# Hybrid pooling and attention block: shift eighths at steps 11 to 26, V's bias by one-column products, w_out's quarters in another order

## What is computed

```python
mod = silu_c @ w_ada[l] + b_ada[l]                      # (B, 6D)
sh_m, sc_m, gt_m, sh_f, sc_f, gt_f = jnp.split(mod[:, None, :], N_MOD, axis=-1)
h = rmsnorm(x, g_pre_mix[l]) * (1 + sc_m) + sh_m
hc = rmsnorm(ctx, g_pre_mix[l]) * (1 + scc_m) + shc_m
p, q1, q2, k1, k2, v = project(h, w_in[l])
...
attn = diff_attend_blocked(q1, q2, k1_all, k2_all, v_all, lam)
attn = rmsnorm(attn, g_subln[l]) * (1 - lambda_init)
pool = pool_mixer(p, w_pool[l], pool_scale[l])
mix = jnp.concatenate([pool, attn.reshape(b, n, ATTN_WIDTH)], axis=-1) @ w_out[l]
x_new = x + gt_m * rmsnorm(mix, g_post_mix[l])
h2 = rmsnorm(x_new, g_pre_ffn[l]) * (1 + sc_f) + sh_f
x_new = x_new + gt_f * rmsnorm(swiglu(h2, w_gate_up[l], w_down[l]), g_post_ffn[l])
```

## Time and profile before

| | us |
|---|---|
| median of 3 runs | 1827.84 (1826.86 to 1827.89) |
| profiled execution, its own time | 1834.15 |
| its span, slowest core (2) | 1832.6 |
| spans of the 8 cores | 1820.8 to 1832.6 |
| TensorE busy | 1731.5 |
| VectorE, ScalarE, GpSimd busy | 624.0, 511.2, 133.0 |

### The profile page before, as it was taken

How to read it: one execution, slowest core, us unless ns; L and a number is a source line. 1 busy time by engine, 2 the same in 40 slices (tenths; PEclk the granted TensorE clock), 3 DMA queues, 4 the chain that set the end, 5 groups by cost and what they waited for, 6 DMA issues and landing times.

```text
span 1832.6 us, 28161 instructions; the slowest of 8 cores (1820.8 to 1832.6 us)
## 1 busy us (share of the span) xinstructions
PE 1731.5 (94%) x11377; PEld 889.6 (49%) x11377; DVE 624.0 (34%) x1360; ACT 511.2 (28%) x794; POOL 133.0 (7%) x147
## 2 busy tenths in 40 slices
PE   1389999999999999989999999999999999999998
PEld 1245545545567676644444444444444444444443
DVE  2124576677545454545521232231110110101023
ACT  2044210000499999925520000000000000101011
POOL 1000000000010111100001111100000000000000
PEclk9599999999999999999999999999999999999999
DMA  9988961045436758674599789757467643544556
GB/s 190 164 205 210 182 116 23 1 63 88 84 60 113 137 96 140 107 147 151 144 163 114 96 114 126 99 75 112 60 81 92 79 86 64 88 70 74 85 146 230
DMA packets 153615, 205.10 MB, mean 112 GB/s; under 512 B 3312, under 2 KB 129680, under 8 KB 146576
## 3 DMA queue, kind: packets, MB, share of 16 engines
q0 software_dynamic: 144368, 145.24, 54.4%
q1 hardware_dynamic: 9120, 58.06, 9.7%
HBM read 331.72 MB, written 16.79 MB: 190 GB/s over the span
## 4 chain that ended last, share of the span: by engine, by line
PE 88%; DMA 6%; another core or an unknown queue 3%; DVE 1%; ACT 1%; issue 1%; SPq 0%; DVEq 0%; POOL 0%; ACTq 0%; POOLq 0%
PE ps L315 87%; DMA arena<-xa 2%; DMA arena<-w_out 2%; PE ps L319 1%; DMA arena<-w_ada 1%; DMA arena<-w_dn 1%; ACT arena L288 1%; DVE arena L298 0%; DVE arena L303 0%; ACT sml L288 0%; DVE arena L306 0%; DVE arena L294 0%; SPq L322 0%; DVE sml L309 0%
## 5 line engine op out<-in xcount | busy, mean ns | idle before, releaser
L315 PE MATMUL ps<-arena 128*128 128x512 bf16 (+2 forms) x9547 | 1683.0, 338 | 20.5 <-DMA arena<-w_out 6.2
L315 PEld LDWEIGHTS ps<-arena 128*128 128x128 bf16 x9547 | 811.7, 98 | 845.8 <-issue 100.7
L288 ACT ACTIVATE arena<-ps 128x1024 bf16<-128x1024 f32 (+5 forms) x500 | 395.3, 838 | 1125.0 <-PE ps L315 1122.4
L294 DVE TENSOR_TENSOR arena<-arena,ps 128x512 bf16<-128x512 f32 (+1 forms) x90 | 61.1, 679 | 491.2 <-PE ps L315 489.9
L303 DVE SCALAR_TENSOR_TENSOR arena<-arena,sml 128x128 f32<-128x128 f32 (+3 forms) x239 | 120.0, 527 | 47.4 <-POOL sml L789 20.8
L294 DVE TENSOR_TENSOR arena<-ps,arena 128x512 f32<-128x512 f32 (+1 forms) x81 | 54.6, 674 | 230.5 <-ACT arena L288 212.0
L294 DVE TENSOR_TENSOR arena<-arena 128x512 f32<-128x512 f32 (+7 forms) x128 | 113.9, 890 | 9.2 <-DVE arena L303 1.4
L319 PE MATMUL ps<-identsb,arena 128*128 128x128 bf16 x499 | 42.2, 232 | 45.4 <-DVE arena L298 28.4
L315 PE MATMUL ps<-cpair,arena 128*128 128x1 bf16 (+1 forms) x1280 | 57.5, 164 | 27.4 <-DMA arena<-w_ada 27.4
L322 POOL DMA_DIRECT2D arena<-w_gu x44 | 50.5, 1150 | 423.5 <-PE ps L315 423.5
L288 ACT ACTIVATE arena<-arena 128x2048 bf16<-128x2048 f32 x27 | 51.5, 1908 | 81.7 <-DVE arena L294 43.2
(11 more groups left out here) (53 smaller groups left out, 225.9 us busy)
## 6 DMA issues: line engine op xcount, KB each, us to landing
arena<-w_gu POOLq DMA_DIRECT2D x44, 1024.0 KB, 14.1
arena<-w_ada POOLq DMA_DIRECT2D x32, 1024.0 KB, 13.2
arena<-xa SPq DMA_DIRECT2D x27, 1024.0 KB, 10.9
arena<-w_dn POOLq DMA_DIRECT2D x16, 1408.0 KB, 11.1
arena<-w_in POOLq DMA_DIRECT2D x6, 2048.0 KB, 19.6
arena<-w_ada POOLq DMA_DIRECT2D x4, 2048.0 KB, 51.3
arena<-w_out POOLq DMA_DIRECT2D x4, 2048.0 KB, 18.0
xscr<-arena SPq DMA_DIRECT2D x8, 1024.0 KB, 4.8
```

The lines of the kernel that those rows point to most:

```text
L288: P.op("act", lambda e: e.activation(out, in_, func, **kw), rd, wr)
L294: P.op("dve", lambda e: e.tensor_tensor(out, a, b, op), [a, b], [out])
L315: P.op("pe", lambda e: e.matmul(out, lhsT, rhs, start=start, stop=stop, skip_group_check=skip), [lhsT, rhs], [out], signal=signal)
```

## The change

1. The eighths of the shift stand behind steps 11, 12, 15, 17, 19, 21, 23 and 26. The x load of tile 6 waits for the third quarter of V's weights only.
2. V's bias: 128 products of one column (the shift as one bf16 column per kc, V's weights stationary) write 8 columns of bank 6. These are scaled, split into three bf16 parts, transposed behind head 0 of K, summed on 8 partitions, stored to DRAM and loaded as a row on all partitions into `bvrow`.
3. The late pool products move from steps 0, 3, 5, 7, 9 of the attention to steps 4, 6, 8, 10, 12, 14; no units of `fill` stand in the first round. So the last unit stands in round 14 behind its step 9, not its step 3. The fifth exponential buffer and the mixer gate's row `GT_m` move to free places.
4. For tile 0 the output projection takes quarters 2, 1, 3 for all four column blocks and then quarter 0; the other tiles take 2, 1, 3, 0 within each block.

```diff
-            dma("sp", xs, xa[i * 128:(i + 1) * 128, :], after=[V_AB[:, 12:16, :]] if late else ())
+            dma("sp", xs, xa[i * 128:(i + 1) * 128, :], after=[V_AB[:, 8 if i == 6 else 12:12 if i == 6 else 16, :]] if late else ())
...
-        shq = {13 + 2 * e: e for e in range(8)}
+        shq = {s_: e for e, s_ in enumerate((11, 12, 15, 17, 19, 21, 23, 26))}
...
-        def bias_v(c2, wslot, b):
-            for kc in range(16):
-                mm(bank(b), shrep[:, kc, :], wslot[:, kc, :], kc == 0, kc == 15, signal=(kc == 15))
-            cp(bvt[:, c2 * 512:(c2 + 1) * 512], bank(b))
+        def bias_v(c2, wslot):
+            for h in range(4):
+                for kc in range(16):
+                    mm(bank(6)[:, 4 * c2 + h:4 * c2 + h + 1], wslot[:, kc, h * 128:(h + 1) * 128], shc[:, kc:kc + 1],
+                       kc == 0, kc == 15, signal=(h == 3 and kc == 15), skip=True)
+
+        def bias_row():
+
+            ts(bcol, bank(6)[:, 0:8], sc1(S_LAM + 6), None, ALU.mult)
+            for k in range(3):
+                cp(bpart[:, k, :], bcol)
+                if k < 2:
+                    tt(bcol, bcol, bpart[:, k, :], ALU.subtract)
+
+        def bias_store():
+            v = bankbf(4)
+            for k in range(3):
+                tp(v[0:8, k * 128:(k + 1) * 128], bpart[:, k, :], signal=(k == 2))
+            cp(brow[0:8, :], v[0:8, 256:384])
+            tt(brow[0:8, :], brow[0:8, :], v[0:8, 128:256], ALU.add)
+            tt(brow[0:8, :], brow[0:8, :], v[0:8, 0:128], ALU.add)
+            P.dma("sp", lambda e: e.dma_start(out=bvs[0].rearrange("(c p) -> c p", p=128), in_=brow[0:8, :]),
+                  [brow[0:8, :]], [("bv", 0)])
...
-        ts(bvrow, bvt, sc1(S_LAM + 6), None, ALU.mult)
+        dma("sp", bvrow, bvs[0].partition_broadcast(128), rd=[("bv", 0)])
...
-            if g == 0:
-                pool_mm(1, (2,), late=True)
             PV(g)
-            if g == 0:
-                pool_mm(1, (3,), late=True)
-            if g in (3, 5, 7, 9):
-                pool_mm(0, [(g - 3) // 2], late=True)
+            if g in (4, 6):
+                pool_mm(1, [g // 2], late=True)
+            if g in (8, 10, 12, 14):
+                pool_mm(0, [g // 2 - 4], late=True)
...
-            if (it > 0 and 3 <= kc <= 13) or (it == 0 and kc > 11):
+            if it > 0 and 3 <= kc <= 13:
                 fill(1)
...
-        def o_mm(t, n):
-            for kc in range(16):
-                mm(bank(ob(t, n)), mixT(kc)[:, t * 128:(t + 1) * 128], w_o[kc // 4][:, kc % 4, n * 512:(n + 1) * 512],
-                   kc == 0, kc == 15, signal=(kc == 15))
+        WQ = (2, 1, 3, 0)
+
+        def o_mm(t, n, qs=WQ):
+            for q in qs:
+                for k in range(4):
+                    mm(bank(ob(t, n)), mixT(4 * q + k)[:, t * 128:(t + 1) * 128], w_o[q][:, k, n * 512:(n + 1) * 512],
+                       q == WQ[0] and k == 0, q == WQ[3] and k == 3, signal=(k == 3))
...
+        for q in WQ[:3]:
+            for n in range(4):
+                o_mm(0, n, (q,))
         for t in range(8):
             for n in range(4):
-                o_mm(t, n)
+                o_mm(t, n, WQ if t else WQ[3:])
```

More of the change, by code:

```diff
@@ L212, in build_nc @@
     xscr = nc.dram_tensor("xscr", [NOWN, D], F32, kind="Internal").ap()
+    bvs = nc.dram_tensor("bvs", [1, 1024], F32, kind="Internal").ap()
     gts = nc.dram_tensor("gts", [2, D], F32, kind="Internal").ap()
@@ L238, in build_nc @@
         P.space("gt", 2, 1)
+        P.space("bv", 1, 1)
         def region(off, nelem, dt):
@@ L484, in add_shift @@
                 ts(o, o, modc[:, 16 + kc:17 + kc], None, ALU.add)
-        shrep = region(KT0, 16 * 128, BF16).rearrange("p (c m) -> p c m", c=16)
-        bvt = region(X0 + 16384, 1024, F32)
-        def bias_v(c2, wslot, b):
-            for kc in range(16):
-                mm(bank(b), shrep[:, kc, :], wslot[:, kc, :], kc == 0, kc == 15, signal=(kc == 15))
-            cp(bvt[:, c2 * 512:(c2 + 1) * 512], bank(b))
+        shc = sc1(244, 8).bitcast(BF16)
+        bcol = sml2[:, 128:136]
+        bpart = sml2[:, 136:148].bitcast(BF16).rearrange("p (k c) -> p k c", k=3)
+        brow = sml2[:, 160:288]
+        def bias_v(c2, wslot):
[18 more added lines that the diff above has]
+                  [brow[0:8, :]], [("bv", 0)])
         gsub = sml2[:, 0:128]
@@ L536, in build_nc @@
             if s == 31:
-                cp(shrep, modc[:, 16:32].unsqueeze(2).to_broadcast([128, 16, 128]))
+                cp(shc, modc[:, 16:32])
             if 28 <= s < 32:
@@ L545, in build_nc @@
             if s == 33:
-                bias_v(0, V_A, 6)
+                bias_v(0, V_A)
                 dma("sp", ropt, rope_d.rearrange("j p t -> p j t"))
             if s == 34:
-                bias_v(1, V_B, 3)
+                bias_v(1, V_B)
+        bias_row()
         add_shift(hT_oth, 0, 256)
@@ L597, in build_nc @@
                 turned(KT[:, h, k0:k0 + n], w, h % 4, src, lo, n, tok)
+            if h == 0:
+                bias_store()
         dma("pool", Q_1, w_in_v[:, :, 1536:2048])
@@ L683, in build_nc @@
         load_ada(3)
-        pbuf = [region(o, 1024, BF16) for o in (HW + 16384, HW + 18432, HW + 20480, HW + 22528, X0 + 23040)]
-        GT_m = region(HW + 24576, 2048, F32)
+        pbuf = [region(o, 1024, BF16) for o in (HW + 16384, HW + 18432, HW + 20480, HW + 22528, HW + 24576)]
+        GT_m = region(X0, 2048, F32)
         GT_f = region(X0, 2048, F32)
```

## The result

The changed kernel takes 1823.84 us (median of 10 runs, 1822.02 to 1825.63), the kernel before 1827.87 in the same runs: ratio 0.9977 (95% interval 0.9968 to 0.9986), 4.0 us less. Forecast were 15.7 less, in a range of 8 to 23 less.

A forecast was written before the change was run, and what follows sets the result against it. TensorE was taken as the bound, working nearly all the time, so only its work or few idle gaps pay. Terms -8.1 - 3.1 - 2.0 - 2.5 = -15.7 us took the median 1827.84 to 1812; range 1805 to 1820.

The forecast's parts named there:

- Part 1: Output projection's head: new order of w_out's quarters removes the 6.17 us wait and low clock; -8.1 us.
- Part 2: V's bias: 128 one-column products at 27 ns replace 32 products of 512 columns; net -3.1 us.
- Rival (c): V's bias: one-column products cost 98 ns each, +9.0 us on the forecast, 1821 us; chance 0.05.
- Part 3: Attention's head: later pool products and moved fills remove ScalarE's 2.51 us pause at exponential 4; -2.0 us.
- Part 4: V's projection: earlier eighths of the shift and earlier x tile of chain 6; -2.5 us, from -9 to +6.
- I take -0.5: V's projection: x tile fetched after the third weight quarter delays the fourth but brings the transposes forward; -0.5 us.
- I take -2.0: V's projection: eighths issued earlier use half-idle DMA engines and shorten TensorE's waits and low clock; -2.0 us.
- rival (a): V's projection: eighths stay the bound, wanted earlier from full DMA engines; 0 to +6 instead of -2.5 us; chance 0.26.

The follow-up runs named there:

- without part 3: Changed kernel with late pool products, fills and the two moved buffers put back as before: ratio 0.9971 to the kernel before.
- shifted kernels: Two of K's product groups written as halves, in the changed kernel (ratio 0.9970) and in it with old eighths and old x load (0.9935).
- half tile: Kernel before plus bias, pool and output-projection changes and two K groups halved; half of chain 6's x tile loads behind V's third weight quarter: ratio 0.9951.
- parts 1 to 3: Changed kernel with eighths and tile 6's x load put back as before: ratio 0.9940 to the kernel before, -9.9 us on the cores' mean.
- changed, old x tile: Changed kernel with tile 6's x load behind V's fourth weight quarter again, moved eighths kept: ratio 0.9940 to the kernel before, -9.6 us on the cores' mean.
- parts 1 to 3 with the two split groups: Changed kernel with old eighths and old x load, two of K's groups of 16 products of 512 columns written as 32 of 256: ratio 0.9935.

## Why the prediction was wrong

**Part 1 held.** -8.1 was forecast; 7.65 us go between the two transposes and 7.0 in the time. The wait for w_out was nearly as long on all cores (4.7 to 6.2 us), so the slowest core's row spoke for all.

**Part 2 held.** -3.1 forecast, -3.33 in the stretch, -2.9 in the time. Rival (c) is out: 64 products of one column in 1.75 us, 27 ns each. The Trainium skill ("TensorE: Matmul & The Clock Gate", "LDWEIGHTS (loading the stationary operand)") gives a load of 128 columns 107 ns, and a single load takes about that here, 98 ns on average. But the loads overlap, with one product every 27 ns: adding them up one after the other, as rival (c) did, is what the trace doesn't bear out.

**Part 3 held at its place and was lost behind it.** The head of the attention is 1.7 us faster at exponential 20 (2.0 forecast), and alone the part gives 1.2. (The forecast's own steps put exponential 13 at 509.0, not 508.8: six and a half steps of 1.10 us behind 501.9.) In the changed kernel the attention is no shorter: part 2's additional instructions and part 3's missing ones together move the boundaries of 256 instructions into the one-column groups. Shifting them back gives 1.9 us of attention; this term was missing from the sum. It does not explain every kernel: without part 3 no boundary lies there, and the attention is as long (270.7 us), of which the slower head is 1.7.

**Part 4 is the failed step.** Forecast -2.5 (-9 to +6), measured +6.2 ± 0.6 (shifted kernels with and without it, same chip). Two steps in it were wrong. First, "up to 1.5 us later there, up to 3.2 earlier at the transposes ... I take -0.5" for the x tile: it is 3.9 us later at the fourth quarter and 0.4 earlier behind it, +3.7 to +5.3 in the time. I had read the idle DMA of 100 to 102 us in the earlier trace rows as free capacity; it is idle there because everything has landed, and the tile was moved from behind this gap into the full stretch ahead of it, where TensorE was already waiting for the last bytes. The wait of 1.47 us in the earlier trace rows said so: what ends it is the DMA itself. The Trainium skill's rule ("DMA: Bandwidth & Descriptors", "Queues, rings and completion order"), engines taking turns between the queues, agrees with the tile's bytes among the quarter's last packets and with the half tile's 9.9 us; the prediction named it and let it undo no more than its 0.5 us. Second, "I take -2.0" for the eighths: they cost 2.1 ± 0.5 us at the kernel before and 0.3 ± 0.7 at parts 1 to 3 (changed, old x tile). The half-idle 140 to 150 us was used (DMA share 0.55 before, 1.02 after), but each eighth from 2 on was wanted two steps, 7 us, earlier in a stretch whose engines were full behind 150 us. So TensorE's wait for eighths didn't shrink, and a term that the sum didn't have came to it: the x tiles behind the eighths come later, and TensorE waits 1.1 us more for them. That is near rival (a), "0 to +6 instead of -2.5", at 0.26: its reason, eighths wanted sooner from full engines, is the smaller part of what the eighths did (0.5 us of waits against the 1.1), and only with the x tile does part 4 come to its upper end.

**The sum.** -7.0, -2.9 and -1.2 for parts 1 to 3, +6.2 for part 4 and +1.0 ± 0.7 for the stalls are -3.9; -4.0 was measured. With some 1.2 us of error in the sum the agreement is closer than the terms deserve. That the profile of before was a long execution did little, as terms and not totals were subtracted, except in part 4, where each of core 2's two waits (3.17 and 3.47 us) was the longest of its kind on the eight cores.

A version that beats both kernels came of it: parts 1 to 3 with the two split groups, 1819.09 us against 1830.87 (ratio 0.9935, 0.9916 to 0.9954).

## What to carry to other kernels

When TensorE waits for a transfer and the DMA engines are full up to its end, nothing may be put ahead of it, however idle the engines are behind it: price a moved load by its bytes at the place where it now passes. When loads are chained (buffer q frees q+2), moving the first ones earlier also moves the date by which all later ones are wanted, and what shares the engines with them comes later. And a term read from the slowest core is worth most when the other cores show the same row.

## What the hardware showed unexpectedly

TensorE's instructions arrive in packets of 16 KB, 256 instructions, one ahead of each boundary, through the same DMA engines as the weights. Beside full weight loads a packet can come late, and TensorE then stands 0.2 to 1.6 us, mostly where instructions are short (27 ns products with their loads). In the changed kernel this is 1.65 us a core from 500 to 760 us, besides 1.7 us a core at the granted clock of 0.50 behind 520 us, of which before had none. So a change in the number of instructions far ahead can move such stalls in or out. What decides how early a packet is asked for is open: kernels without a boundary in the groups of twelve short products had between 0.21 and 0.95 us of stalls.
